# Dense weight products of a transformer block: plain fp32 in place of three fp32r products on split halves

## The chip, the cores and the metric

The kernel runs on one core of one Trainium2 chip, as one launch. The metric is the device time of that launch in microseconds, lower is better. TensorE (PE) multiplies, VectorE (DVE) and ScalarE (ACT) move and compute elementwise, GpSimd (POOL) does small work and issues the gathers, SyncE (SP) issues the weight loads.

## The reference

One transformer block, batch 1, 256 tokens, width 2048, all in fp32:

```python
xn = rms_norm(x, norm_mix_g); z = xn @ w_in            # 2048 x (5632 + 48 + 4096)
# differential attention (8 heads) and NSA attention (16 heads) on z, gated
h  = x + mix(o_da @ w_branch_da, o_nsa @ w_branch_nsa, gates) @ w_out
h += memory_cross_attention(rms_norm(h), rms_norm(mem), w_xq, w_xkv, w_xo)
q  = rms_norm(h) @ peer_wq                              # 2048 x 2048
e  = top 16 of 16384 experts for each of 256 tokens and 8 heads
out = rms_norm(h + sum_k softmax(score) * gelu(U[e_k] . xn) * V[e_k])
```

The dense products are `x @ w_xkv, w_in, w_branch_*, w_out, w_xq, w_xo, peer_wq`; the expert rows U[e] and V[e] are gathered from memory.

## The kernel before

Tokens are on partitions in two halves (C = 2 of 128). A dense product is cut into output tiles of 512 columns (NW), and a tile into eight pieces (PIECES) of 256 rows of the weight, 512 KB each; a piece holds KS = 2 blocks of 128 rows. So a tile takes 8 x 2 x 2 = 32 products of a 128x128 stationary operand (the transposed activations) with 128x512 weights. The tiles are numbered: `T_KV` (2 tiles, memory keys and values), `T_QKV` (11), `T_NG` (one narrow tile of 48 columns), `T_BG` (8, branch gates), `T_BR` (4), `T_WO` (4), `T_XQ` (1): 30 full tiles, 960 products. The tiles of `w_xo` and `peer_wq` that follow are already multiplied as plain fp32, straight from the landed pieces (`xo_pass`, L1098; `h0_piece`, `h1_piece`; `raw_tile_piece`, L1174).

For the 30 tiles SP loads each piece into `wraw`, a ring of WR = 4 slots (L416). ACT copies it to fp32r, the high half (`hi`, L1322); DVE subtracts that from the raw piece, the low half (`lo`, L1753); both go to the ring `ws`, AHEAD = 3 pieces before they are used. The activations are kept as a pair as well: after the transposes on PE, ACT writes the high and DVE the low half into `orr`, `xr` or `xr2` (L1335 and L1762, `mix_hi`/`mix_lo`, `x2_hi`/`x2_lo`). PE then makes each product from three fp32r matmuls into one bank, in `part`:

```python
nc.tensor.matmul(dst, hi, w_h, start=..., stop=False)   # L749
nc.tensor.matmul(dst, hi, w_l, start=False, stop=False) # L750
last = nc.tensor.matmul(dst, lo, w_h, ...)              # L751
```

`xq_piece` (L1029 to L1031) and the narrow tile (L818 to L820) do the same. Order is by program order of each engine and semaphores: `w_landed` (a slot has its piece), `w_hi` and `w_split` (halves made), `w_used` (PE has done with a piece, both token halves). SP's next load into a slot waits for `w_split`; ACT's `hi` waits for `w_used`.

The stages follow each other on PE: the memory tiles, the 11 projection tiles, the narrow tile and the compression (L829), attention, whose small matmuls (L851, L858, L867, L727, L932) alternate with the pieces of the eight gate tiles (`fill`), the branch tiles, `w_out` with the residual on DVE (L2032), the cross-attention query `T_XQ`, cross attention and `w_xo`, `peer_wq`, and last the expert phase: gathers of U rows (L604) for dot products on DVE (L2252) and of V rows (L613) for matmuls with a diagonal (`v_slot`, L1205).

Of the kernel before, what the change touches and what calls it, by code (L numbers as in the profile page):

```python
# [32 lines left out]
F32R = mybir.dt.float32r  # L33
# [12 lines left out]
WR = 4  # L46
AHEAD = 3
MIX_AFTER = 2
EPS = 1e-6
# [35 lines left out]
H_MEM, H_X, H_OT, H_MIX, H_X2, H_OX, H_X3 = 0, 8, 16, 24, 32, 40, 42  # L85
# [75 lines left out]
def block_program(nc, x, mem, positions, norm_mix_g, w_in, lq1, lk1, lq2, lk2, subln_g, cmp_pos, ck1, ck2,  # L161
# [3 lines left out]
    with ctx:  # L165
# [21 lines left out]
        ws = at_kb("ws", 16, [P, WR, 2, KS, NW], F32R)  # L187
        xr = at_kb("xr", 48, [P, 2, KT, S], F32R)
# [3 lines left out]
        orr = at_kb("orr", RES_KB, [P, 2, KT, S], F32R)  # L192
        xr2 = at_kb("xr2", 80 + 32, [P, 2, KT, S], F32R)
# [139 lines left out]
        w_hi, w_split, w_used = sem("w_hi"), sem("w_split"), sem("w_used")  # L333
        hi_done = sem("hi_done")
# [64 lines left out]
        def _(sp):  # L399
# [313 lines left out]
        def _(pe):  # L713
# [96 lines left out]
            for n in range(PIECES):  # L810
                pe.wait_ge(w_split, T_NG * PIECES + n + 1 + WR)
                if n == 0:
                    pe.wait_ge(acc_free[0], T_NG + 1)
                for k in range(KS):
                    kk = n * KS + k
                    w_h, w_l = (ws[:, n % WR, t, k, 0:NG_COLS] for t in range(2))
                    dst = B[0][0:NG_COLS, 0:S]
                    nc.tensor.matmul(dst, w_h, xr[:, 0, kk, :], start=(kk == 0), stop=False)  # L818
                    before = nc.tensor.matmul(dst, w_h, xr[:, 1, kk, :], start=False, stop=False)
                    last = nc.tensor.matmul(dst, w_l, xr[:, 0, kk, :], start=False, stop=(kk == KT - 1))  # L820
                if n == PIECES - 1:
                    before.then_inc(acc0_ready, 1)
# [147 lines left out]
            def branch_part(i, n, groups=None):  # L970
                if n < 4:
                    part(i + T_BR, i + T_BR, n, orr[:, :, 0:8, :], final=3, groups=groups)
                else:
                    part(i + T_BR, i, n, orr[:, :, 8:16, :], bank=4, first=4, groups=groups)
# [45 lines left out]
            def xq_piece(n, c):  # L1020

                if c == 0:
                    pe.wait_ge(w_split, T_XQ * PIECES + (n + 1 + WR))
                if n == 0:
                    pe.wait_ge(acc_free[c], T_XQ + 1)
                for k in range(KS):
                    x_h, x_l = (xr2[:, t, n * KS + k, c * P:(c + 1) * P] for t in range(2))
                    w_h, w_l = (ws[:, n % WR, t, k, :] for t in range(2))
                    nc.tensor.matmul(B[c], x_h, w_h, start=(n == 0 and k == 0), stop=False)  # L1029
                    nc.tensor.matmul(B[c], x_h, w_l, start=False, stop=False)  # L1030
                    last = nc.tensor.matmul(B[c], x_l, w_h, start=False, stop=(n == PIECES - 1 and k == KS - 1))  # L1031
# [10 lines left out]
            for n in range(WR):  # L1042
# [6 lines left out]
            for n in range(WR, PIECES):  # L1049
# [159 lines left out]
            xq_piece(WR, 1)  # L1209
            xq_piece(WR + 1, 1)  # L1210
            qx_transposes(0)
            xq_piece(WR + 2, 1)
# [5 lines left out]
            xq_piece(WR + 3, 1)  # L1218
# [78 lines left out]
        def _(act):  # L1297
# [5 lines left out]
            act.sem_inc(w_split, WR)  # L1303
# [20 lines left out]
            def next_cols(n, cols, following):  # L1324

                return cols if n + AHEAD < PIECES else following

# [4 lines left out]
            def evac_hi(n, number, dst):  # L1332

                act.wait_ge(tp_ready[n % 2], n // 2 + 1)
                A(dst, four(n), ACT.Copy).then_inc(hi_done, 1)  # L1335

# [3 lines left out]
            def quarter_hi(base, q, dst):  # L1340
                for c in range(C):
                    evac_hi(base + 2 * q + c, 0, dst[:, 0, 4 * q:4 * q + 4, c * P:(c + 1) * P])
# [19 lines left out]
            hi(-3, 0)  # L1362
            quarter_hi(G_MEM, 0, orr)
            hi(-2, 0)
            quarter_hi(G_MEM, 1, orr)
            hi(-1, 0)
            for k in range(PIECES - 1):
                hi(k, T_KV)
                if k in (1, 3):
                    quarter_hi(G_MEM, 2 + k // 2, orr)  # L1370
                if k in (4, 5):
                    squares(k - 4, ssq[:, k - 4:k - 3], mn[:, k - 4, :], square_a)
            for c in range(C):
                copy_acc(c, T_KV, T_KV, stage_a[:, c, :], 0)
            hi(PIECES - 1, T_KV)
# [3 lines left out]
            for k in range(PIECES):  # L1379
                hi(k, T_KV + 1)  # L1380
                if k == 1:
                    for c in range(C):
                        evac(G_MK + c, kxT[:, :, c * P:(c + 1) * P], four(G_MK + c))
                if 2 <= k < 6:
                    quarter_hi(G_X, k - 2, xr)
                if k in (3, 4):
                    for q in range(4):
                        act.wait_ge(x_landed[q], 16)
                    squares(2 + k - 3, ssq[:, 2 + k - 3:3 + k - 3], xn[:, k - 3, :], square_a)
# [5 lines left out]
            def qkv_tile(i):  # L1395
                for n in range(PIECES):
                    hi(n, i + T_QKV)
# [9 lines left out]
            for last in range(T_CMP + 2 - T_QKV, N_QKV):  # L1407
                for n in range(PIECES):
                    hi(n, T_QKV + last, next_cols(n, NW, NG_COLS) if last == N_QKV - 1 else NW)
# [3 lines left out]
            for n in range(PIECES):  # L1413
                hi(n, T_NG, next_cols(n, NG_COLS, NW))
            acc_wait(1, T_NG, T_NG)
            A(gnT[:, :], B[0][0:NG_COLS, 0:S], ACT.Copy).then_inc(acc_free[0], 1)
            act.sem_inc(acc_free[1], 1)
# [13 lines left out]
            A(lamb[:, 2:4], lamb[:, 0:2], ACT.Exp).then_inc(lam_exp, 1)  # L1431

# [24 lines left out]
            with act.Fori(0, N_G) as g:  # L1457
                for j in range(2):
# [12 lines left out]
                    tile = step + T_BG  # L1471
                    exps(U[0], 0, nks[0])
                    exps(U[1], 1, nks[1])
                    hi(0, tile)
                    copy_pt(U[0], 0, nt[0])
                    hi(1, tile)
# [4 lines left out]
                    hi(2, tile)  # L1481
                    exps(U[3], 3, nks[3])
                    copy_pt(U[2], 2, nt[2])
                    hi(3, tile)
# [4 lines left out]
                    hi(4, tile)  # L1489
                    exps(U[5], 5, nks[5])  # L1490
                    copy_pt(U[4], 4, nt[4])
                    hi(5, tile)
                    copy_pt(U[5], 5, nt[5])
                    hi(6, tile)
                    hi(7, tile)
# [4 lines left out]
            def mix_hi(i):  # L1500
                for c in range(C):
# [3 lines left out]
            for n in range(PIECES):  # L1505
                if n < 4:
                    quarter_hi(G_OT, n, orr)
                hi(n, T_BR)
            with act.Fori(1, N_BR) as i:
                for n in range(PIECES):  # L1510
                    if n == MIX_AFTER:
                        mix_hi(i - 1)
                    hi(n, i + T_BR)
            for n in range(PIECES):
                if n == MIX_AFTER:
                    mix_hi(N_BR - 1)
                hi(n, T_WO)
            def x2_hi(i):
                for c in range(C):
                    act.wait_ge(tp_ready[c], i + (G_X2 // 2 + 1))  # L1520
                    A(xr2[:, 0, bass.ds(i * 4, 4), c * P:(c + 1) * P], four(c), ACT.Copy).then_inc(hi_done, 1)

            with act.Fori(1, N_WO - 1) as i:
                for n in range(PIECES):
# [868 lines left out]
```

## Time and profile before

| | us |
|---|---|
| median of 3 timed runs (2191.33 to 2194.05) | 2192.86 |
| span of the profiled execution, first to last instruction | 2192.2 |
| PE busy in it | 1887.3 |
| DVE busy | 1292.6 |
| ACT busy | 583.2 |
| mean DMA rate | 320 GB/s |

The profiled execution's span is 0.66 us under the median, and the record gives no other time for it, so sums made against the span are read as sums against the median too. An interval between two instructions' starts tells how long one holds PE; a matmul's own duration is longer, since matmuls are pipelined and their ends are modelled. Busy time is a union of such durations.

### The profile page before, as it was taken

How to read it: one execution, taken by the hardware profiler on the slowest of the kernel's cores; microseconds unless marked ns; L12 is line 12 of the kernel's file. 1: busy time of each engine (PE TensorE's matmuls, PEld its weight loads, DVE VectorE, ACT ScalarE, POOL GpSimd, SP SyncE). 2: the span in 40 equal slices, each digit the busy share in tenths (PEclk: the TensorE clock that was granted, in tenths of full speed). 3: DMA queues.
4: the chain of work that ended last, by engine and by line, in shares of the span. 5: the costliest groups of instructions: out<-in, count | busy, mean ns of one | idle time of the engine just before them, and what ended most of it. 6: DMA issues, size and time to landing. Idle time of an engine off the chain costs nothing.

```text
span 2192.2 us, 22286 instructions
## 1 busy us (share of the span) xinstructions
PE 1887.3 (86%) x6607; PEld 1118.5 (51%) x6607; DVE 1292.6 (59%) x2173; ACT 583.2 (27%) x1058; POOL 716.3 (33%) x621
## 2 busy tenths in 40 slices
PE   8999999999999999999987777777777777777776
PEld 7888887777788886544433222222222222222222
DVE  6554557777766554876365566466466556556444
ACT  5544445455544442121111111111111111111101
POOL 1000101010000001445464454455455455455542
PEclk9999999999999999999999999999999999999999
DMA  8667744343456665999999999999999999999997
GB/s 295 182 177 207 229 141 116 115 115 115 124 169 211 213 226 194 391 413 412 411 412 421 421 422 422 422 422 422 422 421 422 421 422 421 423 421 422 422 421 328
DMA packets 163553, 700.86 MB, mean 320 GB/s; under 512 B 15616, under 2 KB 23840, under 8 KB 97200
## 3 DMA queue, kind: packets, MB, share of 16 engines
q0 software_dynamic: 74144, 537.32, 59.1%
q1 hardware_dynamic: 89216, 162.68, 23.7%
q8 instruction: 24, 0.39, 0.1%
q10 hardware_dynamic: 144, 0.26, 0.0%
q14 instruction: 25, 0.20, 0.0%
HBM read 698.11 MB, written 2.10 MB: 319 GB/s over the span
## 4 chain that ended last, share of the span: by engine, by line
PE 53%; DMA 37%; issue 4%; DVE 3%; POOL 1%; ACT 1%; POOLq 0%; DVEq 0%; SPq 0%; ACTq 0%
DMA v_ring<-in_peer_v_dram,idx_v 29%; PE banks L1205 11%; PE banks L749 10%; PE banks L751 9%; PE banks L750 9%; DMA big<-in_peer_u_dram,idx_u 6%; PE banks L1174 4%; DVE big L2252 2%; PE banks L867 2%; PE banks L727 1%; PE banks L851 1%; DMA wraw<-in_w_xkv_dram 1%; PE banks L858 1%; POOL v_ring L613 1%; PE banks L1117 1%
## 5 line engine op out<-in xcount | busy, mean ns | idle before, releaser
L1205 PE MATMUL banks<-v_ring,kxT 128*128 128x512 f32 x1920 | 887.2, 606 | 271.5 <-DMA v_ring<-in_peer_v_dram,idx_v 267.1
L2252 DVE SCALAR_TENSOR_TENSOR big<-big,xn 128x2048 f32<-128x2048 f32 x256 | 586.8, 2292 | 411.9 <-DMA big<-in_peer_u_dram,idx_u 403.5
L1205 PEld LDWEIGHTS banks<-v_ring,kxT 128*128 128x128 f32 x1920 | 349.5, 191 | 806.5 <-ACT kxT L1659 391.7
L604 POOL DMA_INDIRECT big<-in_peer_u_dram,idx_u x256 | 357.7, 1397 | 235.1 <-DVE big L2252 140.6
L613 POOL DMA_INDIRECT v_ring<-in_peer_v_dram,idx_v x240 | 286.3, 1193 | 388.6 <-PE banks L1205 347.0
L1753 DVE TENSOR_TENSOR ws<-wraw,ws 128x1024 fp32r<-128x1024 f32 (+1 forms) x248 | 294.8, 1195 | 189.7 <-ACT ws L1322 187.5
L1659 ACT ACTIVATE kxT<-ident,ga 128x128 f32<-128x128 f32 x240 | 95.4, 401 | 962.6 <-PE banks L1205 955.7
L1322 ACT ACTIVATE ws<-wraw 128x1024 fp32r<-128x1024 f32 (+1 forms) x248 | 254.8, 1032 | 226.1 <-PE banks L751 203.8
L749 PE MATMUL banks<-ws,xr 128*128 128x512 f32 x736 | 294.3, 400 | 0.9 <-DVE h L2032 0.9
L751 PE MATMUL banks<-ws,xr 128*128 128x512 f32 x736 | 287.3, 390 | 0.0
L750 PE MATMUL banks<-ws,xr 128*128 128x512 f32 x736 | 286.6, 389 | 0.0
L749 PEld LDWEIGHTS banks<-ws,xr 128*128 128x128 f32 x736 | 138.2, 188 | 33.2 <-issue 2.7
L751 PEld LDWEIGHTS banks<-ws,xr 128*128 128x128 f32 x736 | 138.1, 188 | 30.1
L750 PEld LDWEIGHTS banks<-ws,xr 128*128 128x128 f32 x736 | 138.4, 188 | 26.9
L559 POOL TENSOR_TENSOR rstd<-msq,nhalf 128x1 f32<-128x1 f32 x9 | 5.0, 558 | 314.2 <-DVE msq L1740 220.7
L593 POOL TENSOR_TENSOR ms<-ms,nhalf 128x2 f32<-128x2 f32 x8 | 5.5, 690 | 244.6 <-DVE ms L1939 244.6
L749 PE MATMUL banks<-ws,orr 128*128 128x512 f32 x192 | 76.5, 398 | 5.1 <-DVE orr L1762 2.4
L751 PE MATMUL banks<-ws,orr 128*128 128x512 f32 x192 | 75.0, 390 | 0.0
L750 PE MATMUL banks<-ws,orr 128*128 128x512 f32 x192 | 74.7, 389 | 0.0
L570 POOL COPY att<-big 128x256 f32<-128x256 f32 x8 | 5.8, 767 | 194.5 <-DVEq L1881 194.5
L2259 DVE TENSOR_TENSOR ga<-act_u,gw 128x16 f32<-128x16 f32 x16 | 2.8, 175 | 106.2 <-ACT act_u L1653 106.2
L1438 ACT ACTIVATE att<-att,nmx 128x128 f32<-128x128 f32 (+1 forms) x96 | 42.7, 446 | 56.3 <-DVE nmx L1906 56.3
(301 smaller groups left out, 1538.4 us busy)
## 6 DMA issues: line engine op xcount, KB each, us to landing
wraw<-in_w_in_dram SPq DMA_DIRECT2D x152, 512.0 KB, 3.7
wraw<-in_w_out_dram SPq DMA_DIRECT2D x32, 512.0 KB, 4.0
wraw<-in_w_xkv_dram SPq DMA_DIRECT2D x16, 512.0 KB, 7.0
wraw<-in_w_branch_da_dram SPq DMA_DIRECT2D x16, 512.0 KB, 3.7
wraw<-in_w_branch_nsa_dram SPq DMA_DIRECT2D x16, 512.0 KB, 4.2
wq<-in_peer_wq_dram SPq DMA_DIRECT2D x16, 512.0 KB, 21.1
wraw<-in_w_xq_dram SPq DMA_DIRECT2D x8, 512.0 KB, 3.6
wb<-in_peer_wq_dram SPq DMA_DIRECT2D x8, 512.0 KB, 8.0
```

Source lines behind the costliest of these rows:

```text
L604: nc.gpsimd.indirect_dma_start(u_ring[:, r, :], None, peer_u[0], bass.IndirectOffsetOnAxis(ap=idx_u[par][:, j:j + 1], axis=0)).then_inc(u_ ...
L613: nc.gpsimd.indirect_dma_start(v_ring[:, r, :], None, peer_v[0], bass.IndirectOffsetOnAxis(ap=idx_v[par][:, j:j + 1], axis=0)).then_inc(v_ ...
L749: nc.tensor.matmul(dst, hi, w_h, start=(n == first and k == 0), stop=False)
L750: nc.tensor.matmul(dst, hi, w_l, start=False, stop=False)
L751: last = nc.tensor.matmul(dst, lo, w_h, start=False, stop=(n == final and k == KS - 1))
L867: last = nc.tensor.matmul(dst, a, v, start=(n == 0), stop=(n == len(terms) - 1))
L1174: last = nc.tensor.matmul(B[c], xf[:, n * KS + k, c * P:(c + 1) * P], raw_pieces[raw_slot(g)][:, k, :], start=(n == 0 and k == 0), stop=(n ...
L1205: last = nc.tensor.matmul(V_BANKS[c][n], diag[:, r, :], v_ring[:, r, n * NW:(n + 1) * NW], start=(first and j == 0), stop=(final and j == ...
L1322: A(ws[:, q % WR, 0, :, 0:cols], wraw[:, q % WR, :, 0:cols], ACT.Copy).then_inc(w_hi, 1)
L1659: A(diag[:, j % RING, :], ident[:, :], ACT.Copy, scale=ga[:, par, j:j + 1]).then_inc(diag_ready, 1)
L1753: V.tensor_tensor(ws[:, q % WR, 1, :, 0:cols], wraw[:, q % WR, :, 0:cols], ws[:, q % WR, 0, :, 0:cols].bitcast(F32), ALU.subtract).then_in ...
L2252: V.scalar_tensor_tensor(out=u_ring[:, r, :], in0=u_ring[:, r, :], scalar=1.0, in1=xn3[:, par, :], op0=ALU.mult, op1=ALU.mult, accum_out=d ...
```

## The change

All halves go. `xr`, `orr` and `xr2` hold one fp32 copy; ACT evacuates the transposes of the first token half and DVE those of the second. `ws` is gone, and `wraw` takes its room as a ring of eight slots, one for each piece of a tile. PE waits for `w_landed` itself and makes each product with one plain fp32 matmul from `wraw`. SP's load into a slot waits for `w_used` of the piece eight before. The pieces of `w_xo`, which land in the same room, each wait for the `T_XQ` piece of the same number to be used for both token halves. The gate tiles' second accumulator is now handed over after `rope_done`. `XQ_BOTH = 4` keeps the order of the query tile that WR gave before.

```diff
-WR = 4
-AHEAD = 3
+WR = PIECES
+XQ_BOTH = 4
...
-        ws = at_kb("ws", 16, [P, WR, 2, KS, NW], F32R)
-        xr = at_kb("xr", 48, [P, 2, KT, S], F32R)
+        xr = at_kb("xr", 48, [P, KT, S])
...
             def load(n, tile, src, cols=NW):
-                sp.wait_ge(w_split, tile * PIECES + (n + 1))
+                sp.wait_ge(w_used, tile * PIECES + (n + 1))
                 sp.dma_start(wraw[:, n % WR, :, 0:cols], src).then_inc(w_landed[n % WR], 16)
...
-            for i in range(WR):
-                sp.wait_ge(w_split, T_XQ * PIECES + WR + i + 1 + WR)
-                xo_piece(i)
-            for i in range(WR, PIECES):
-                sp.wait_ge(w_used, T_XQ * PIECES + WR + (i - WR) // 2 + 1 + WR)
+            for i in range(PIECES):
+                sp.wait_ge(w_used, T_XQ * PIECES + WR + i + 1)
                 xo_piece(i)
...
-                pe.wait_ge(w_split, tile * PIECES + (n + 1 + WR))
+                pe.wait_ge(w_landed[n], tile * 16 + 16)
...
                     for k in range(KS):
-                        hi, lo = (lhs[:, t, (n - first) * KS + k, c * P:(c + 1) * P] for t in range(2))
-                        w_h, w_l = (ws[:, n % WR, t, k, 0:cols] for t in range(2))
-                        dst = B[bank + c][:, 0:cols]
-                        nc.tensor.matmul(dst, hi, w_h, start=(n == first and k == 0), stop=False)
-                        nc.tensor.matmul(dst, hi, w_l, start=False, stop=False)
-                        last = nc.tensor.matmul(dst, lo, w_h, start=False, stop=(n == final and k == KS - 1))
+                        last = nc.tensor.matmul(B[bank + c][:, 0:cols], lhs[:, (n - first) * KS + k, c * P:(c + 1) * P], wraw[:, n, k, 0:cols],
+                                                start=(n == first and k == 0), stop=(n == final and k == KS - 1))
...
-            def hi(n, tile, cols=NW):
-                q = n + AHEAD
-                act.wait_ge(w_landed[q % WR], tile * (16 * PIECES // WR) + 16 * (q // WR + 1))
-                act.wait_ge(w_used, tile * PIECES + (q + 1))
-                A(ws[:, q % WR, 0, :, 0:cols], wraw[:, q % WR, :, 0:cols], ACT.Copy).then_inc(w_hi, 1)
...
+            act.wait_ge(rope_done, 2)
+            act.sem_inc(acc_free[1], 1)
...
-            def mix_hi(i):
-                for c in range(C):
-                    act.wait_ge(tp_ready[c], i + (G_MIX // 2 + 1))
-                    A(xr[:, 0, bass.ds(i * 4, 4), c * P:(c + 1) * P], four(c), ACT.Copy).then_inc(hi_done, 1)
+            def mix_0(i):
+                act.wait_ge(tp_ready[0], i + (G_MIX // 2 + 1))
+                A(xr[:, bass.ds(i * 4, 4), 0:P], four(0), ACT.Copy).then_inc(tp_free[0], 1)
...
-            def lo(n, tile, cols=NW):
-                q = n + AHEAD
-                dve.wait_ge(w_hi, tile * PIECES + (q + 1))
-                V.tensor_tensor(ws[:, q % WR, 1, :, 0:cols], wraw[:, q % WR, :, 0:cols], ws[:, q % WR, 0, :, 0:cols].bitcast(F32),
-                                ALU.subtract).then_inc(w_split, 1)
...
+            def quarter_1(base, q, dst):
+                n = base + 2 * q + 1
+                dve.wait_ge(tp_ready[1], n // 2 + 1)
+                V.tensor_copy(dst[:, 4 * q:4 * q + 4, P:S], B[3].rearrange("p (t s) -> p t s", t=4)).then_inc(tp_free[1], 1)
```

Every call of `hi` and `lo` is deleted with them. Nothing from `xo_pass` on changes.

## Rows read from the trace of the kernel before

**Rows 1.** Page, part 4: shares of the chain that ended last, by line.
```profile
DMA v_ring<-in_peer_v_dram,idx_v 29%; PE banks L1205 11%; PE banks L749 10%; PE banks L751 9%; PE banks L750 9%; DMA big<-in_peer_u_dram,idx_u 6%; PE banks L1174 4%; DVE big L2252 2%; PE banks L867 2%; PE banks L727 1%; PE banks L851 1%; DMA wraw<-in_w_xkv_dram 1%; PE banks L858 1%; POOL v_ring L613 1%; PE banks L1117 1%
```

**Rows 2.** Busy time by stage; columns: stretch and length, engines, clock, DMA share, GB/s.
```profile
11.00:41.40 30.40, 25.80 (x123) 20.59 (x123) 18.88 (x24) 15.59 (x20) 1.10 (x2) 1.00 1.02 347
41.40:67.90 26.50, 26.43 (x137) 22.27 (x137) 20.80 (x29) 18.94 (x25) 0.00 (x0) 1.00 0.54 160
67.90:309.80 241.90, 241.33 (x1073) 199.80 (x1072) 123.83 (x149) 108.52 (x117) 6.85 (x10) 1.00 0.64 190
309.80:325.90 16.10, 15.08 (x135) 14.62 (x134) 8.56 (x34) 9.46 (x20) 4.65 (x6) 1.00 0.73 232
325.90:607.80 281.90, 281.55 (x1545) 221.16 (x1544) 209.62 (x557) 149.98 (x357) 23.98 (x42) 1.00 0.40 116
607.80:703.40 95.60, 95.60 (x462) 80.15 (x462) 61.70 (x73) 40.76 (x46) 0.00 (x0) 1.00 0.58 181
703.40:796.60 93.20, 91.84 (x418) 75.02 (x417) 54.26 (x58) 41.09 (x45) 0.00 (x0) 1.00 0.65 215
796.60:821.90 25.30, 25.28 (x119) 21.01 (x120) 10.99 (x17) 9.87 (x20) 1.08 (x2) 1.00 0.84 275
821.90:900.00 78.10, 71.62 (x302) 50.34 (x301) 44.83 (x104) 19.26 (x51) 15.56 (x13) 0.96 0.65 244
```

**Rows 3.** Page, part 5: the two operations that make the weights' halves.
```profile
L1753 DVE TENSOR_TENSOR ws<-wraw,ws 128x1024 fp32r<-128x1024 f32 (+1 forms) x248 | 294.8, 1195 | 189.7 <-ACT ws L1322 187.5
L1322 ACT ACTIVATE ws<-wraw 128x1024 fp32r<-128x1024 f32 (+1 forms) x248 | 254.8, 1032 | 226.1 <-PE banks L751 203.8
```

**Rows 4.** PE's instructions in order of time, steady projection tiles, first and last.
```profile
119.80 0.39 PE L750 MATMUL banks<-ws,xr 128*128 128x512 f32 x1
...
125.92 0.39 PE L750 MATMUL banks<-ws,xr 128*128 128x512 f32 x1
```

**Rows 5.** Groups by line and form on PE: records of fp32r and of plain fp32.
```profile
L749 PE MATMUL banks<-ws,xr 128*128 128x512 f32 x736 | 294.3, 400 | 0.9 <-DVE h L2032 0.9
L749 PE MATMUL banks<-ws,orr 128*128 128x512 f32 x192 | 76.5, 398 | 5.1 <-DVE orr L1762 2.4 <-ACT big L1354 1.6 <-DVE ws L1753 1.1
...
L1098 PE MATMUL banks<-wq,big 128*128 128x512 f32 x64 | 28.2, 594 | 0.0
...
L1029 PE MATMUL banks<-ws,xr 128*128 128x512 f32 x32 | 12.9, 403 | 0.4 <-DVE h L2032 0.4
```

**Rows 6.** Chain that ended last, in order of time: start, length, what.
```profile
315.64 7.10 PE banks L829 x64
...
892.85 3.45 PE banks L1145 x16
...
908.62 20.62 PE banks L1174 x48
```

**Rows 7.** PE's instructions in order of time, the edges of one attention fill.
```profile
354.62 0.39 PE L751 MATMUL banks<-ws,xr 128*128 128x512 f32 x1
354.94 0.43 PE L867 MATMUL banks<-vc,att 15*128 x2
355.30 0.66 PE L867 MATMUL banks<-big,att 128*128 x4
355.80 0.61 PE L858 MATMUL banks<-ident,att 128*128 128x128 f32 x4
356.16 0.47 PE L749 MATMUL banks<-ws,xr 128*128 128x512 f32 x1
356.48 0.39 PE L750 MATMUL banks<-ws,xr 128*128 128x512 f32 x1
```

**Rows 8.** DMA issues: kind, count, size, median us from issue to landing.
```profile
wraw<-in_w_in_dram SPq DMA_DIRECT2D x152, 512.0 KB, 3.7
...
h<-in_x_dram SPq DMA_DIRECT2D x1, 2048.0 KB, 8.9
```

More of the change, by code:

```diff
@@ L191, in block_program @@
         big = at_kb("big", 80, [P, BIG])
[L192 to L193 removed]
+        orr = at_kb("orr", RES_KB, [P, KT, S])
+        xr2 = at_kb("xr2", 80 + 32, [P, KT, S])
         mng_t = at_kb("mng", 48, [P, C, D])
@@ L815, in _ @@
                     kk = n * KS + k
[L816 to L822, printed above, removed]
+                    last = nc.tensor.matmul(B[0][0:NG_COLS, 0:S], wraw[:, n, k, 0:NG_COLS], xr[:, kk, :], start=(kk == 0), stop=(kk == KT - 1))
+                    if n == PIECES - 1 and k == 0:
+                        last.then_inc(acc0_ready, 1)
                 last.then_inc(w_used, 1)
@@ L971, in branch_part @@
                 if n < 4:
-                    part(i + T_BR, i + T_BR, n, orr[:, :, 0:8, :], final=3, groups=groups)
+                    part(i + T_BR, i + T_BR, n, orr[:, 0:8, :], final=3, groups=groups)
                 else:
-                    part(i + T_BR, i, n, orr[:, :, 8:16, :], bank=4, first=4, groups=groups)
+                    part(i + T_BR, i, n, orr[:, 8:16, :], bank=4, first=4, groups=groups)
             def x2_transposes(i):
@@ L1026, in xq_piece @@
                 for k in range(KS):
[L1027 to L1031, printed above, removed]
+                    last = nc.tensor.matmul(B[c], xr2[:, n * KS + k, c * P:(c + 1) * P], wraw[:, n, k, :],
+                                            start=(n == 0 and k == 0), stop=(n == PIECES - 1 and k == KS - 1))
                 if c == 1:
@@ L1040, in qx_transposes @@
                 transposes(G_QX + c, [(stage_b[:, c, t * P:(t + 1) * P], t * P) for t in range(X_H)])
-            for n in range(WR):
+            for n in range(XQ_BOTH):
                 if n == MIX_AFTER:
@@ L1048, in _ @@
                     xq_piece(n, c)
-            for n in range(WR, PIECES):
+            for n in range(XQ_BOTH, PIECES):
                 if n % 2 == 0:
@@ L1359, in evac @@
                 A(dst, src, ACT.Copy).then_inc(tp_free[n % 2], 1)
[L1362 to L1372, printed above, removed]
+            for q in range(4):
+                quarter_0(G_MEM, q, orr)
+            for c in range(C):
+                squares(c, ssq[:, c:c + 1], mn[:, c, :], square_a)
             for c in range(C):
                 copy_acc(c, T_KV, T_KV, stage_a[:, c, :], 0)
-            hi(PIECES - 1, T_KV)
             for c in range(C):
@@ L1378, in _ @@
                 act.sem_inc(act_steps, 1)
[L1379 to L1389, printed above, removed]
+            for c in range(C):
+                evac(G_MK + c, kxT[:, :, c * P:(c + 1) * P], four(G_MK + c))
+            for q in range(4):
+                quarter_0(G_X, q, xr)
+                act.wait_ge(x_landed[q], 16)
+            for c in range(C):
+                squares(2 + c, ssq[:, 2 + c:3 + c], xn[:, c, :], square_a)
             for c in range(C):
@@ L1509, in _ @@
-            with act.Fori(1, N_BR) as i:
[L1510 to L1521, printed above, removed]
@@ new lines, in _, with x2_0 @@
+            for q in range(4):
+                quarter_0(G_OT, q, orr)
+            with act.Fori(1, N_BR) as i:
+                mix_0(i - 1)
+            mix_0(N_BR - 1)
+            def x2_0(i):
+                act.wait_ge(tp_ready[0], i + (G_X2 // 2 + 1))
+                A(xr2[:, bass.ds(i * 4, 4), 0:P], four(0), ACT.Copy).then_inc(tp_free[0], 1)
+            with act.Fori(1, N_WO - 1) as i:
+                x2_0(i - 1)
+            x2_0(N_WO - 2)
+            act.wait_ge(h_done, 2 * N_WO - 2)
@@ L1543, in x_query @@
+            for c in range(C):
+                squares_h(2, c, False)
+            x2_0(N_WO - 1)
+            for c in range(C):
+                act.wait_ge(h_done, 2 * N_WO - 1 + c)
+                squares_h(2, c, True)
             def x_query(c):
@@ L1777, in x_gain @@
                 gain_quarter(xn, xg, gmix, q)
[L1779 to L1797 removed]
+            for q in range(4):
+                mem_gain(q)
+                quarter_1(G_MEM, q, orr)
+            for c in range(C):
+                mean_square(0, c, 1 + c)
+            x_gain(0)
             dve.wait_ge(tp_ready[0], G_POS // 2 + 1)
@@ L1802, in _ @@
             V.tensor_copy(keysT[:, :, :].rearrange("p t n -> p (t n)"), B[3][:, 0:2 * P]).then_inc(tp_free[1], 1)
-            for n in range(PIECES):
-                lo(n, T_KV + 1)
-                if n < 3:
-                    x_gain(n + 1)
-                if 2 <= n < 6:
-                    quarter_lo(G_X, H_X, xr, n - 2)
+            for q in range(4):
+                if q < 3:
+                    x_gain(q + 1)
+                quarter_1(G_X, q, xr)
             dve.wait_ge(small_landed, 16 * N_SMALL)
@@ new lines, in _ @@
+                    for t in range(2):
+                        for c in range(C):
+                            dve.wait_ge(tp_free[c], (G_CMP + 2 * t + c) // 2 + 2)
+                        for odd in range(2):
+                            rows = slice(64 * odd, 64 * odd + 64)
+                            for lh in range(2):
+                                seen = xsT[rows, t, :, 16 * lh:16 * lh + 240].rearrange("p g (n l o) -> p o l g n", o=2, l=8)[:, odd]
+                                place = posT[rows, 16 * lh:16 * lh + 16].rearrange("p (l o) -> p o l", o=2)[:, odd]
+                                last = V.tensor_tensor(blk[rows, t, 8 * lh:8 * lh + 8, :, :], seen,
+                                                       place.unsqueeze(2).unsqueeze(3).broadcast_to([64, 8, N_G, N_CMP]), ALU.add)
+                        last.then_inc(blk_ready, 1)
@@ L1881, in _ @@
                     dve.sem_inc(rope_done, 1)
-                if tiles == N_QKV:
-                    for n in range(PIECES - AHEAD, PIECES):
-                        lo(n, T_NG, NW)
             for c in range(C):
@@ L1978, in compressed_out @@
                         last.then_inc(cp_ready, 1)
-                    tile = step + T_BG
-                    SM(0), SM(1), difference(0), compressed_in(), difference(1), lo(0, tile), SM(2), lo(1, tile)
-                    EV(0), SM(3), lo(2, tile), EV(1), compressed_out(), SM(4), lo(3, tile)
-                    SM(5), EV(2), lo(4, tile), EV(3), lo(5, tile), head_norm(), EV(4), lo(6, tile), lo(7, tile), EV(5)
+                    SM(0), SM(1), difference(0), compressed_in(), difference(1), SM(2)
+                    EV(0), SM(3), EV(1), compressed_out(), SM(4)
+                    SM(5), EV(2), EV(3), head_norm(), EV(4), EV(5)
                 link.end(N_G)
             def branch_tile(i):
-                for c in range(C):
-                    for n in range(2 * c, 2 * c + 2):
-                        if isinstance(i, int):
-                            quarter_lo(G_OT, H_OT, orr, n)
-                        elif n == MIX_AFTER:
-                            mix_lo(i - 1)
-                        lo(n, i + T_BR)
+                if isinstance(i, int):
+                    for q in range(4):
+                        quarter_1(G_OT, q, orr)
+                else:
+                    mix_1(i - 1)
                 for c in range(C):
@@ L2002, in branch_tile @@
                                            op0=ALU.add, op1=ALU.mult).then_inc(acc_free[c], 1)
-                    lo(4 + c, i + T_BR)
-                for n in range(6, PIECES):
-                    lo(n, i + T_BR)
                 for c in range(C):
@@ L2046, in _ @@
                 branch_tile(i)
-            for n in range(PIECES):
-                if n == MIX_AFTER:
-                    mix_lo(N_BR - 1)
-                lo(n, T_WO)
+            mix_1(N_BR - 1)
             dve.wait_ge(h_landed, 16)
@@ L2054, in _ @@
             with dve.Fori(1, N_WO) as i:
-                for n in range(PIECES):
-                    if n == MIX_AFTER:
-                        x2_lo(i - 1)
-                    lo(n, i + T_WO)
+                x2_1(i - 1)
                 residual(i)
-            for n in range(PIECES - AHEAD):
-                if n == MIX_AFTER:
-                    x2_lo(N_WO - 1)
-                lo(n, T_XQ)
+            x2_1(N_WO - 1)
             mean_squares_h(2)
```

131 lines of the change are left out of this document (15 added, 116 removed).

## The prediction

> **What bounds the kernel now.** I read the page's chain of waits first [rows 1]. Two things fill it: the gathers of the last phase, and the three lines of the fp32r products (L749 to L751, 28% of the span together). The split lines L1753 and L1322 are not among its larger shares. So the question is what PE does before the gathers begin. The busy time by stage answers it [rows 2]: from 41.4 to 821.9 us PE's busy time falls short of the length by 3.4 us in all, and the granted clock is 1.00, which is the higher level, 2.4 GHz. Only the first stretch has idle time worth naming (4.6 us), and there the DMA runs at 347 GB/s. The DVE and ACT columns of the same rows are far from full. What they do for a piece, 1.195 us on DVE and 1.032 us on ACT [rows 3], is hidden behind the piece's twelve fp32r matmuls on PE: ACT waited 203.8 us for PE's L751 and DVE 187.5 us for ACT, so the split chain waits for PE and not the reverse. I conclude that taking the splits away frees engines that set nothing, and that the time follows what a product costs on PE.
>
> **The product, before.** In the steady stretch 27 matmuls lie between the starts 119.80 and 125.92 [rows 4]; 6.12 / 27 = 0.2267 us each, three to a product: 0.680 us. The durations of 0.39 overlap and are not the cost. A tile is 32 products, 21.76 us; eleven tiles make 239.4 us, and the projection stage lasts 241.9 with a few transposes in it [rows 2]. The price holds over the stage.
>
> **The product, after.** The kernel has the new form already, in the last dense tiles: same stationary 128x128, same 512 columns, two k blocks a piece. The trap is in the counting. `xo_pass` makes 8 x 4 = 32 products in the code, and the trace has 64 records of its line L1098 [rows 5]; L749, one fp32r matmul, has 736 records for 23 tiles x 32 products. So one plain fp32 matmul is two records. The chain shows 48 records of L1174 in 20.62 us with nothing between them [rows 6]: 0.4296 us a record, 0.859 us a product. A product thus goes from 0.680 to 0.859 us, +0.179.
>
> The Trainium skill, in "FP8 and Floating Point Precision", section "TensorE Precision Notes", says that true fp32 takes four passes through the array. At one column a cycle and 2.4 GHz that is an estimate of 4 x 512 / 2.4 = 853 ns for a product; by that rule, the trace agrees (859). A second page prices it differently and is weighed among the rivals.
>
> **The sum, stage by stage.** Full tiles hold 736 + 192 + 32 = 960 products [rows 5].
>
> - First memory tile. 32 x 0.179 = +5.7. Taken away are PE's waits ahead of L749 on `orr` (2.4), on ACT's copy of the accumulator (1.6) and on `ws` (1.1) [rows 5], 5.1 in all: the operands' evacuation is one copy on each of two engines in place of two steps in a row, the squares on ACT no longer stand behind splits, and a landed piece needs no split. The loads keep their place in SP's queue behind the same quarters of `mem`, so they land no later; at 347 GB/s they can't land much earlier either. Net +0.6. Bounds: +5.7 if another wait replaces these, 0 if all are gone and the slower PE hides a little more.
> - Second memory tile, 11 projection, 8 gate, 4 branch, 4 output tiles and the query tile: 29 x 32 = 928 products, all in stages where PE has no idle time to absorb them: 928 x 0.179 = +166.1.
> - Narrow tile. It runs from 309.8 [rows 2] to about 315.5, before L829 at 315.64 [rows 6]: 5.7 us for 16 products of 256 columns. Plain fp32 at 256 columns is 3.45 us for 16 records [rows 6], 0.216 each; 32 records make 6.9. So +1.2.
> - Edges of the 64 attention fills. The gap from the last fp32r matmul to L867 is 0.32 and not 0.227, and the first matmul after the transposes holds 0.32 too [rows 7]: 0.09 at each end, at most 64 x 0.18 = 11.5 us. Part of it is the true cost of the small instruction before, and part the change of operand rows, both of which stay. I take -3, with 0 and -11.5 as the ends. Idle time that the longer fills could still hide is 0.35 us in this stage [rows 2], nothing.
> - Between the output tiles PE waits for DVE's residual L2032, 0.9 + 0.4 us [rows 5]. PE goes on with the second token half meanwhile, which grows by the same 0.179 a product, and DVE has no split in front of the residual. The wait goes, and a little of the modelled ends with it: -2. Bounds 0 and -3.
> - Copies on ACT and DVE that remain: about as many as before and half as long in sequence, behind 3.4 us pieces. Cost nothing; were that cover gone, each group of transposes would show one, half a split's 1.195 us [rows 3] for half its columns, 0.6 us.
> - Loads. PE takes 512 KB in 4 x 0.859 = 3.44 us, 153 GB/s, less than the 190 that the projection stage draws [rows 2]. A slot is refilled when PE has used it, seven pieces or 24 us before it is needed, against 3.7 us to land and 8.9 for the 2 MB of `h` [rows 8], behind which piece 7 of the first output tile still queues. Nothing late. Likewise the pieces of `w_xo`: the last is issued when the query tile ends and is used three `xo_pass` later, after 3 x 4 x 0.859 = 10.3 us and more. The broadcast behind it in SP's queue is one 512 KB piece later, inside the same slack. Hidden; if not, 1 to 3 us once.
> - Everything after 821.9 us is unchanged work in unchanged order: it moves as a block. DVE and ACT lose 295 and 255 us of busy time [rows 3], which the chain did not hold.
>
> Sum: 0.6 + 166.1 + 1.2 - 3 - 2 = +162.9. The third decimal of the product matters: two records in 0.858 in place of 0.859 take 1 us off. I round to +161. On 2192.2 us, and on the median, that is **2353.5 us**, 7.4% slower.
>
> **Rivals.**
>
> Faster, because a plain product costs 0.430 and not 0.859. If the two records were one product's two token halves, or a second record an artefact, each product would fall from 0.680 to 0.430: 960 x -0.250 = -240, 1952 us. It decides the sign from below 0.680 us a product. For it: one record alone does take 0.430. Against it: the code's count of L1098 against its 64 records [rows 5]. Two in a hundred.
> The Trainium skill, in "Perfetto Trace Analysis", section "Engine Utilization", halves the output rate of 307.2 G elements/s for fp32 low-high; read as the rate of a whole product, an estimate of 512 x 128 / 153.6 G = 427 ns, this rival's price. The trace agrees with it for one record only.
>
> The clock drops. Plain fp32 would keep PE at work without pause for 950 us, and if it were granted less for parts of that, products would double to 1.72 us there. Against it: 20.62 us of L1174 at full rate and 1.00 in every dense stage now. For it: 0.96 in the stretch 821.9 to 900 [rows 2], though that stretch holds 6.5 us of PE idling. If the dense stages fell to 0.96 the mean cost would be 960 x 0.859 x 0.04 = 33 us more: 2387. Four in a hundred.
>
> Loads or hand-overs come late. The ring now waits for PE itself, and SP's queue is one line: a late `h` load holds the next tile's pieces. Three or four waits of 4 us: +14, 2367. Against it the slack above. Four in a hundred.
>
> The fill edges and small waits give back their whole bound, as everything on PE is then one kind: -8.5 more on the edges, -1 on the residual: 2344. One in ten, and inside my range.
>
> No change, as where plain fp32 would be made of three records or be issued as before: 2192. Against it the two records. Under one in a hundred.
>
> **How the numbers follow.** My forecast has 79 in 100, with its neighbour (2344) 89. The range takes the bounds: low is 2192.2 + 0 + 166.1 + 1.2 - 11.5 - 3 - 1 (the third decimal) = 2344, taken to 2341 for the scatter between runs; high is 5.7 + 166.1 + 1.2 with nothing given back, 173, that is 2365, and reaches to 2367 for the late loads. Outside it lie the clock, the faster rival, no change and what I don't see: about one in ten. Faster by over 0.2%: 0.03, the counting rival and a little. Within 0.2%, about what a measurement of this kernel can tell from no change: 0.01. Slower: 0.96.
>
> **What would show it.** In the profile after, the line of `part` has two records for each product, 1856 over `xr` and `orr`, with starts 0.429 us apart and no wait ahead of them; the projection stage lasts 302 to 305 us; an attention step of 35.2 us takes about 40.5; the first U gather comes about 160 us later, and from there to the end nothing moves. The expert phase keeps its DMA rate. The prediction is wrong if the spacing is not 0.429 in the long stages, if the clock there is not 1.00, or if PE shows waits for `wraw`.

## The result, and the profile after

The changed kernel takes 2354.88 us (median of 4, 2354.01 to 2356.12) against 2193.01 (4 runs, 2191.33 to 2194.05): a ratio of 1.0737, interval 1.0722 to 1.0752. That is 161.9 us more, where 161 were forecast. The profiled execution spans 2351.1 us, 158.9 more than the one before; the two figures differ by the scatter of the runs, which is 2 to 3 us for either kernel.

First the chain that ended last, shares by line, the answer to [rows 1]:

```profile
PE banks L739 34%; DMA v_ring<-in_peer_v_dram,idx_v 28%; PE banks L1187 10%; DMA big<-in_peer_u_dram,idx_u 7%; PE banks L1156 4%; PE banks L852 2%; DVE big L2115 1%; PE banks L720 1%; PE banks L1012 1%; PE banks L836 1%; POOL v_ring L606 1%; PE banks L843 1%; PE banks L1080 1%; PE banks L1099 1%; PE banks L1127 0%
```

L739 is the one matmul of `part`; it stands where L749 to L751 stood with 28%, and the gathers' share has merely shrunk with the longer span. The groups on PE by line and form, beside [rows 5]:

```profile
L739 PE MATMUL banks<-wraw,xr 128*128 128x512 f32 x1472 | 647.1, 595 | 0.0
L739 PE MATMUL banks<-wraw,orr 128*128 128x512 f32 x384 | 167.6, 592 | 0.0
...
L1012 PE MATMUL banks<-wraw,xr 128*128 128x512 f32 x64 | 28.1, 592 | 0.0
```

1472 + 384 = 1856 records for 928 products: two for each, as counted. The last number, PE's idle time ahead of the line, is 0.0 in all three: PE never waits ahead of a dense product, where it waited 5.1 + 0.9 + 0.4 us before. The chain in order of time gives the price over a long stretch, beside [rows 6]:

```profile
66.15 281.55 PE banks L739 x656
```

656 records with nothing between them, 0.4292 us each, 0.858 us a product. Busy time by stage, the same stages as [rows 2] at their new places (the branch and output tiles are left out):

```profile
11.00:41.00 30.00, 30.00 (x90) 14.47 (x89) 7.55 (x14) 6.71 (x9) 1.51 (x2) 1.00 1.05 370
41.00:72.80 31.80, 31.80 (x106) 16.31 (x105) 9.90 (x30) 8.41 (x12) 1.07 (x2) 1.00 0.49 148
72.80:377.60 304.80, 304.23 (x721) 135.24 (x719) 16.18 (x44) 18.80 (x29) 2.79 (x8) 1.00 0.51 147
377.60:395.30 17.70, 16.68 (x119) 13.05 (x119) 3.55 (x26) 5.29 (x12) 1.90 (x6) 1.00 0.69 241
395.30:720.30 325.00, 324.65 (x1288) 173.99 (x1287) 137.13 (x493) 93.66 (x292) 16.54 (x42) 1.00 0.36 102
...
952.50:982.70 30.20, 30.20 (x87) 14.78 (x86) 4.42 (x11) 4.90 (x14) 1.11 (x2) 1.00 0.62 205
982.70:1060.00 77.30, 71.49 (x305) 50.32 (x304) 44.68 (x104) 19.01 (x50) 15.39 (x13) 0.96 0.68 249
```

The DVE column, the third of the busy times, shows the splits gone: 124 us in the projection stage before, 16 now; 210 and 137 in attention. PE's column fills each dense stage, as before, and each stage is longer by its products. The clock is 1.00 throughout, 2.4 GHz, and the one stretch at 0.96 is cross attention, as before; of its two longer waits the one of 3.6 us stays and the other falls from 1.5 to 0.8 us. An attention step takes 325.0 / 8 = 40.6 us, where about 40.5 were forecast, and the gathers run at 421 to 422 GB/s in most slices of either page. The first gather of U rows leaves at 859.1 us before and at 1019.6 after: +160.5. From there to the end it is 1333.1 and 1331.5 us.

### The profile page after: what moved, and what is told of

Read it like the earlier page. It is cut to its first block, busy times and chain, and to the rows that moved or that the text cites. A ratio compares the mean times of both kernels' runs of the same rounds, so it can differ in the third digit from the quotient of the medians.

```text
span 2351.1 us, 19088 instructions
## 1 busy us (share of the span) xinstructions
PE 2051.8 (87%) x5631; PEld 939.8 (40%) x5631; DVE 995.5 (42%) x1905; ACT 333.8 (14%) x790; POOL 711.7 (30%) x621
## 4 chain that ended last, share of the span: by engine, by line
PE 57%; DMA 35%; issue 4%; DVE 2%; POOL 1%; ACT 0%; POOLq 0%; DVEq 0%; ACTq 0%
PE banks L739 34%; DMA v_ring<-in_peer_v_dram,idx_v 28%; PE banks L1187 10%; DMA big<-in_peer_u_dram,idx_u 7%; PE banks L1156 4%; PE banks L852 2%; DVE big L2115 1%; PE banks L720 1%; PE banks L1012 1%; PE banks L836 1%; POOL v_ring L606 1%; PE banks L843 1%; PE banks L1080 1%; PE banks L1099 1%; PE banks L1127 0%
## 5 line engine op out<-in xcount | busy, mean ns | idle before, releaser
L739 PE MATMUL banks<-wraw,xr 128*128 128x512 f32 x1472 | 647.1, 595 | 0.0
L597 POOL DMA_INDIRECT big<-in_peer_u_dram,idx_u x256 | 363.3, 1419 | 229.7 <-DVE big L2115 138.8
L739 PEld LDWEIGHTS banks<-wraw,xr 128*128 128x128 f32 x1472 | 274.2, 190 | 323.8 <-issue 320.3
L739 PE MATMUL banks<-wraw,orr 128*128 128x512 f32 x384 | 167.6, 592 | 0.0
L739 PEld LDWEIGHTS banks<-wraw,orr 128*128 128x128 f32 x384 | 71.6, 190 | 83.7 <-issue 83.7
L1319 ACT ACTIVATE big<-banks,rstd 128x512 f32 (+1 forms) x26 | 17.9, 688 | 303.2 <-PE banks L739 291.1
L1156 PE MATMUL banks<-wq,big 128*128 128x512 f32 x128 | 56.6, 592 | 0.0
L1783 DVE SCALAR_TENSOR_TENSOR att<-banks,causal 128x256 f32<-128x256 f32 (+1 forms) x48 | 26.7, 556 | 51.5 <-PE banks L836 50.4
L1906 DVE SCALAR_TENSOR_TENSOR h<-banks,h 128x512 f32 (+1 forms) x8 | 5.5, 692 | 76.7 <-PE banks L739 76.7
L852 PE MATMUL banks<-big,att 128*128 x240 | 36.1, 281 | 0.0
```

Of the source, the lines that this page charges most:

```text
L597: nc.gpsimd.indirect_dma_start(u_ring[:, r, :], None, peer_u[0], bass.IndirectOffsetOnAxis(ap=idx_u[par][:, j:j + 1], axis=0)).then_inc(u_ ...
L739: last = nc.tensor.matmul(B[bank + c][:, 0:cols], lhs[:, (n - first) * KS + k, c * P:(c + 1) * P], wraw[:, n, k, 0:cols], start=(n == firs ...
L852: last = nc.tensor.matmul(dst, a, v, start=(n == 0), stop=(n == len(terms) - 1))
L1156: last = nc.tensor.matmul(B[c], xf[:, n * KS + k, c * P:(c + 1) * P], raw_pieces[raw_slot(g)][:, k, :], start=(n == 0 and k == 0), stop=(n ...
L1783: V.scalar_tensor_tensor(out=sv, in0=pv, scalar=ATT_SCALE, in1=mask.unsqueeze(1).broadcast_to([P, 2, nk]), op0=ALU.mult, op1=ALU.add).then ...
```

## The experiments

Runs are beside the kernel before on the same chip, whose medians were 2193.0 to 2193.8. "First gather" is the start of the first L604 (or the same statement under its new line number), the end of all that the change touches.

**The product's form alone.** The kernel before with all its splits and waits, one plain matmul on the high halves read as fp32. The narrow tile keeps its three fp32r matmuls:

```diff
-nc.tensor.matmul(dst, hi, w_h, ...); nc.tensor.matmul(dst, hi, w_l, ...); nc.tensor.matmul(dst, lo, w_h, ...)
+last = nc.tensor.matmul(dst, hi.bitcast(F32), w_h.bitcast(F32), ...)
```

> The kernel before with its splits, its rings and all its hand-overs, but each dense product is one plain fp32 matmul on the two high halves read as fp32; the low halves are still made and not used, so the low terms are left out. My theory (the product's price on TensorE is the whole change, 0.859 against 0.680 us): as slow as the changed kernel, 2353 to 2363 us, and at most 5 us above it, because the waits in the first memory tile stay. Rival (the freed VectorE and ScalarE, the eight slots and the single copies are worth something that hid part of a still dearer product): 2370 us or more.

Measured 2352.89 us (4 runs), ratio 1.0729 (1.0711 to 1.0747). The first gather leaves at 1020.2 us, 0.6 us after the changed kernel's. The groups by line on DVE and ACT show that the work is still there:

```profile
L1749 DVE TENSOR_TENSOR ws<-wraw,ws 128x1024 fp32r<-128x1024 f32 (+1 forms) x248 | 294.9, 1194 | 289.9 <-ACT ws L1318 287.6 <-DVE big L1844 1.0
```
```profile
L1318 ACT ACTIVATE ws<-wraw 128x1024 fp32r<-128x1024 f32 (+1 forms) x248 | 253.8, 1028 | 321.1 <-PE banks L749 300.1 <-DMA wraw<-in_w_xkv_dram 8.7 <-PE banks L1027 6.0
```

So 549 us of work on two engines, four raw slots and every hand-over of the pairs came back, and the time did not change by what can be measured. In the first gather this run is 0.6 us later although its narrow tile is 1.4 us shorter, so splits, pairs and ring together are worth about 2 us. Of some 160 us the form of the product is all the rest; its rival, over 2370 us, is out.

**Four fp32r products.** A fourth matmul, low times low:

```diff
+nc.tensor.matmul(dst, lo, w_h, start=False, stop=False)
+last = nc.tensor.matmul(dst, lo, w_l, start=False, stop=...)
-last = nc.tensor.matmul(dst, lo, w_h, start=False, stop=...)
```

> The kernel before with a fourth fp32r matmul, low half times low half, for each of the 960 full products. If a stage lasts as long as its matmuls: +960 x 0.2267 = +218 us, 2411 us, so four fp32r matmuls (0.907 us) come out 46 us above one plain fp32 product (0.859 us). Rival, that the split chain or the loads set the time in part: less than 200 us more.

Measured 2404.96 us (2 runs), ratio 1.0965 (1.0943 to 1.0987): +211, 7 short of the sum, and first gather +210.4. Longer pieces hide most of the waits on splits and residuals, as the plain product does: of the 6.4 us that PE idled ahead of the dense products before, 1.0 are left, on `orr`. Four fp32r matmuls cost 52 us more than one plain product in the same kernel (e1: 2352.89), by the spacings 960 x (0.907 - 0.858) = 47. Plain fp32 is about what four fp32r passes are, a little cheaper, and three of them are cheaper still.

**Two fp32r products, splits kept.** Without the low activations:

```diff
 nc.tensor.matmul(dst, hi, w_h, ...)
-nc.tensor.matmul(dst, hi, w_l, start=False, stop=False)
-last = nc.tensor.matmul(dst, lo, w_h, start=False, stop=...)
+last = nc.tensor.matmul(dst, hi, w_l, start=False, stop=...)
```

> The kernel before without the product of the low activations (two fp32r matmuls a product; that term is left out). A piece then takes 1.81 us on TensorE against 1.195 us on VectorE. My theory: the split chain is still hidden, -218 us, 1975 to 1985 us. Rival: the splits or the slot's cycle of load, high half and low half (about 3.7 + 1.0 + 1.2 us for four slots, 1.5 us a piece) set the time already: over 2000 us.

Measured 2035.11 us (2 runs), ratio 0.9279 (0.9260 to 0.9297). My expectation failed: 159 us less and not 218, and the rival's range was the right one. The groups on PE until 700 us show waits that were not there before, 27 us of them ahead of L749:

```profile
L749 PE MATMUL banks<-ws,xr 128*128 128x512 f32 x736 | 299.9, 407 | 17.6 <-DVE ws L1751 7.5 <-ACT big L1352 6.2 <-DVE h L2030 3.4
...
L749 PE MATMUL banks<-ws,orr 128*128 128x512 f32 x192 | 78.0, 407 | 9.4 <-ACT big L1352 4.0 <-DVE orr L1760 3.4 <-DVE ws L1751 2.1
```

DVE takes 1.2 us for a piece of 1.81, so its mean was no obstacle; its queue was. A chain of rotations holds it at 129 to 134 us, the split stands behind them, and PE stands behind the split. The chain in order of time has it:

```profile
133.19 0.35 DVE big L1846
133.75 1.24 DVE ws L1751
135.03 0.50 PE banks L749
```

That is one place. ScalarE's late accumulator copies (`big`) cost PE as much as the splits do (10.2 and 9.6 us). Up to the end of the query tile PE is busy for 606.9 of 654.6 us:

```profile
11.00:665.60 654.60, 606.87 (x3041) 480.18 (x3042) 502.54 (x937) 393.29 (x644) 36.73 (x62) 0.98 0.68 214
```

That is 47.7 us idle, against 8.0 in the same stages of the kernel before (802.6 of 810.6). The clock also has a part: its mean there is 0.98 and not 1.00.

**One fp32r product, splits kept.** Only `hi` times `w_h`.

> The kernel before with one fp32r matmul a product, high times high; both low terms are left out, all splits are still made. TensorE alone would save 960 x 0.453 = 435 us: 1758 us. My theory: here the split chain and the slot's cycle (load, high, low: about 1.5 us a piece) bind outside attention, and VectorE's own 210 us bind inside it: about 290 us saved, 1880 to 1930 us. Rival, that splits are always hidden: under 1800 us.

Measured 2030.93 us (2 runs, 2022.92 to 2038.93), ratio 0.9258 (0.9222 to 0.9295). With half of the matmuls of the run before it, it gains next to nothing: first gather at 705.1 us against 703.0. Far over my range. The same stages, up to the end of the query tile:

```profile
11.00:667.70 656.70, 491.34 (x2080) 355.70 (x2081) 502.64 (x937) 389.15 (x644) 36.64 (x62) 0.81 0.67 212
```

960 x 0.2267 = 218 us of matmuls were taken out against the run with two. PE's busy time fell by 115.5 us only, and its idle time rose by 117.7: ahead of L749 PE alone waits 39.4 us for DVE's splits and 39.4 for ScalarE's accumulator copies. The other 102 us came back inside PE's busy time. Some of them are modelled ends ahead of the new waits; most go with the granted clock, 0.81 on average where the run with two has 0.98. Dense matmuls start 0.427 us apart in the stretches at the lower level and 0.227 in those at the higher. An estimate from these rows: 0.38 of 656.7 us at the lower level, with PE busy for three quarters of them, cost half of 187 us, 93 us, and 12 us in the run with two. The expectation had no term for the clock. How much of it lies on the path that sets the time was not tested.

**Half the columns, no splits.** The changed kernel with 256 columns in 824 of its 960 products; half of their columns are left out:

```diff
+ends = (n == first and k == 0) or (n == final and k == KS - 1)
+half = slice(0, cols) if ends else slice(k * cols // 2, (k + 1) * cols // 2)
-last = nc.tensor.matmul(B[bank + c][:, 0:cols], lhs[...], wraw[:, n, k, 0:cols], ...)
+last = nc.tensor.matmul(B[bank + c][:, half], lhs[...], wraw[:, n, k, half], ...)
```

> The changed kernel with 256 columns in place of 512 in 824 of the 960 plain products (the first and last of each accumulation stay whole), so half of those products' columns are left out. If each of the two records goes with its columns: 824 x 0.428 = 353 us less, 2002 us, at 1.72 us a piece without any split. Rival, that the loads (512 KB in 1.72 us, 305 GB/s) set the time: over 2020 us.

Measured 2016.41 us (2 runs), ratio 0.9192 (0.9175 to 0.9209), 14 above the sum. First gather 681.7, 337.9 before the changed kernel's where 353 were worked out. PE's waits are short and scattered (4.9 us in attention, 1.1 on the loads of `w_xkv`); they don't add up to the 15, and I leave the rest open. Still, at a piece of 1.72 us the kernel without splits gives up 15 of 353 us, and the kernel with splits at 1.81 us 59 of 218.

**Weights rounded only.** The same two products' worth on PE as in the run with two, but without DVE's subtraction for the weights; their low halves are left out:

```diff
 def lo(n, tile, cols=NW):
-    V.tensor_tensor(ws[:, q % WR, 1, :, 0:cols], wraw[...], ws[...].bitcast(F32), ALU.subtract).then_inc(w_split, 1)
+    pass
...
-A(ws[:, q % WR, 0, :, 0:cols], wraw[:, q % WR, :, 0:cols], ACT.Copy).then_inc(w_hi, 1)
+A(ws[:, q % WR, 0, :, 0:cols], wraw[:, q % WR, :, 0:cols], ACT.Copy).then_inc(w_split, 1)
...
-nc.tensor.matmul(dst, hi, w_l, start=False, stop=False)
```

> The kernel before, with the weights only rounded to fp32r by ScalarE and VectorE's subtraction for them taken out; a product is two fp32r matmuls, high and low half of the activation with the rounded weight, so the weights' low halves are left out. TensorE's work is that of the run with two products, which saved 159 us where its matmuls alone were worth 218. My theory (that run lost its 59 us to VectorE's subtraction standing in line with rotations, residuals and softmax ahead of TensorE): at least 45 of them come back, 1980 to 1992 us. Rival (the slot's cycle of load and rounding, or late copies on ScalarE): 2010 us or more.

Measured 1996.64 us (4 runs), ratio 0.9096 (0.9081 to 0.9111). 38 us of the 59 came back, under my 45 and some 5 us above my range, and some 2 of them belong to the narrow tile, which lost its third product too: the first gather leaves at 661.1, 42 us before that of the run with two. The run doesn't separate DVE's queue from the cycle of a slot: without the subtraction a raw slot is also free earlier, and ScalarE's waits for landings of `w_in` fell from 38.1 to 13.7 us. What is left ahead of L749 is ScalarE's:

```profile
L749 PE MATMUL banks<-ws,xr 128*128 128x512 f32 x736 | 296.1, 402 | 3.8 <-ACT ws L1319 2.4 <-ACT vmem L1351 1.1 <-ACT big L1351 0.2
...
L749 PE MATMUL banks<-ws,orr 128*128 128x512 f32 x192 | 78.3, 408 | 4.9 <-ACT ws L1319 2.6 <-ACT big L1351 1.9 <-issue 0.4
```

**Weights rounded, one product.** All low terms left out.

> As the run before it, with one fp32r matmul a product, the high half of the activation with the rounded weight; all low terms are left out. TensorE alone: 1758 us. My theory: outside attention the loads set the time, 512 KB at 350 to 390 GB/s being 1.35 to 1.5 us a piece against 0.91 on TensorE, and in attention the softmax chain: 1840 to 1890 us. Rival (VectorE's subtraction was not what held the run with one product): 2000 us or more.

Measured 1931.10 us (4 runs), ratio 0.8805 (0.8790 to 0.8820): 100 us below the run with one product and its splits, so the subtraction did hold that one, and 41 above my range. Part of the 100 us came by way of the clock: its mean up to the end of the query tile is 0.92 here and 0.81 there. I had the next bound wrong. It was to be the loads; PE's own waits name ScalarE:

```profile
PE banks L749 <- ACT big L1349: 41.1, 10, 5.5
PE banks L749 <- ACT ws L1317: 34.8, 32, 7.6
```

These are the copies of the accumulators (`big`) and the rounding (`ws`), one engine's queue. Behind it ScalarE itself waits for landings of `w_in` for 35.4 us and of `w_out` for 20.6, so the loads have a part in it. Which of the two would give more was not tried.

**A shorter lead of the ring.** The changed kernel, loads held until four more pieces are used:

```diff
-sp.wait_ge(w_used, tile * PIECES + (n + 1))
+sp.wait_ge(w_used, tile * PIECES + (n + 1 + 4))
```

> The changed kernel with each load of the ring held until four more pieces are used, so that pieces land at most three ahead and only four slots are in use. My theory (24 us of lead were far more than the 3.6 us to land, 3 x 3.44 = 10.3 us still are): the same within 0.2%, 2351 to 2359 us. Rival, that the lead of eight slots kept the price of late loads down: 2365 us or more, with waits for the weight ring on TensorE.

Measured 2353.77 us (4 runs), ratio 1.0733 (1.0715 to 1.0750), the changed kernel's within the scatter. No wait for `wraw` appears on PE. Eight slots bring nothing here that four don't.

**Fewer waits with fp32r.** The kernel before, in another order:

```diff
-                if k in (4, 5):
-                    squares(k - 4, ...)
+                if k in (3, 4):
+                    squares(k - 3, ...)
...
 def residual(i):
     for c in range(C):
+        if c == 1:
+            lo(PIECES - 1, i + T_WO)      # was ahead of residual(i)
```

> The kernel before, with fp32r as it was, but two waits of TensorE taken out by order alone: ScalarE squares the memory rows one piece earlier (wait of 1.6 us at the second memory tile), and VectorE does the residual of the first token half before the last split of an output tile (four waits of about 0.5 us). My theory: 3 to 4 us less, 2189 us, at the edge of what can be measured; the trace shows the waits gone. Rival: the waits are taken over by another engine, same time.

Measured 2190.95 us (11 runs) against 2193.20 (15 runs), ratio 0.9994 (0.9985 to 1.0003): not told from no change. The first gather leaves at 856.7 us, 2.4 earlier. The residual's part of the theory holds, its wait of 0.9 us ahead of L749 [rows 5] is gone:

```profile
L749 PE MATMUL banks<-ws,xr 128*128 128x512 f32 x736 | 294.3, 400 | 0.0
```

The other part does not: PE still waits 1.75 us for ScalarE at the second memory tile.

```profile
40.78 0.47 PE L749 MATMUL banks<-ws,orr 128*128 128x512 f32 x1 [1.75 <-ACT big L1354]
```

## Why the prediction was right

The step that carries it is the price of a product. The stages bear out its terms one by one, each start read from PE's instructions in order of time:

| stage | forecast | measured |
|---|---|---|
| first memory tile, up to the second's start (41.47 to 41.01) | +0.6 | -0.5 |
| second memory tile, projections (to 309.85; to 377.65) | +68.7 | +68.3 |
| narrow tile (to 315.48; to 384.69) | +1.2 | +1.4 |
| compression, up to attention (10.4; 10.6) | 0 | +0.2 |
| attention with 256 fill products (281.9; 325.0) | +45.8 - 3 | +43.1 |
| branch and output tiles (188.8; 231.6) | +45.8 - 2 | +42.8 |
| query tile (25.0; 30.5) | +5.7 | +5.5 |
| after it (1370.6; 1368.6) | 0 | -2.0 |

The stages up to the end of the query tile add up to +160.9, the forecast's terms to +162.8, taken to 161 for the third decimal. That the medians differ by 161.9 is partly luck: the profiled executions differ by 158.9, and the first tile, the output tiles and the end each came out about 1 to 2 us under their terms.

**Product.** 0.858 in place of 0.859 us; the form run shows by itself that this is the change.

**First memory tile.** The waits are gone, and with them a little more than their modelled length: -0.5 lies just outside the bounds of 0 and +5.7. In the form run, where the operands' pairs stay, the wait for `orr` is 1.05 us again and the tile starts at 11.70 against 10.37:

```profile
11.70 3.67 PE L749 MATMUL banks<-ws,orr 128*128 128x512 f32 x8 [1.05 <-DVE orr L1758]
```
```profile
10.37 3.60 PE L739 MATMUL banks<-wraw,orr 128*128 128x512 f32 x8
```

The first line is the form run's, the second the changed kernel's, both from PE's instructions in order of time. The 1.3 us are what the single copies bring there. The reasons given for the rest were not needed. The form run keeps the pairs, the splits and the squares behind them, and yet the second wait for `orr` (1.35 us before), the one for `ws` (1.1) and the one for ACT's accumulator copy (1.6) are gone from it too: a longer product hides them. Nor was 347 GB/s the limit of the loads; the changed kernel draws 370 in this stretch. The form run is no slower at the end than the changed kernel, within scatter.

**Fill edges.** I took 3 of at most 11.5 us. Measured are 2.6: 256 products at the measured 0.178 us are 45.7, and the stage grew by 43.1. The number was right, and where it came from was not. The gap ahead of the attention matmuls [rows 7] stays with plain fp32 on both sides, here as 3.53 us between a fill's start and L852, where its eight records take 3.43:

```profile
425.43 3.60 PE L739 MATMUL banks<-wraw,xr 128*128 128x512 f32 x8
428.96 0.43 PE L852 MATMUL banks<-vc,att 15*128 x2
```

The words on the change of rows hold. A plain record ahead of work on 15 or 64 rows (L852 on `vc`, L836) holds PE 0.52 us and one ahead of work on all 128 rows its steady 0.43; fp32r held 0.32 and 0.23 in the same places, so 0.09 stays in either form. The other edge was in part no cost. Behind transposes the first fp32r matmul held 0.314 us, but the last transpose ahead of it held 0.028 and now holds 0.109: the time has only moved to another instruction. So the edges gave back less than 0.5 us of the 3. The other 2.1 were inside the fills: the 640 fp32r matmuls there started 0.230 us apart on average and not the 0.2267 that the forecast carried over from the projection stage, while plain records keep 0.4292. Why fp32r is slower there was not tested.

**Residual.** The wait went, as forecast, and the stage gave back 2.9 us against 45.7, within the bounds of 0 and -3. In the form run, where DVE still has a split in front of the residual, it is gone too, so the longer second token half is enough.

**Cover.** That the splits lay behind PE was right at 2.72 us a piece, but for the one wait of 1.1 us in the first tile, and the form run shows it at 3.43. But the words "frees engines that set nothing" rested partly on mean times, and that reasoning doesn't carry far: at 1.81 us a piece, with the same 1.2 us a piece on DVE, 59 of the 218 us did not come, and without the subtraction 38 of them did.

**Loads and the rest.** Nothing late, with either lead. The clock rival did not come: 1.00 in every dense stage under 960 x 0.858 = 824 us of plain fp32 products. The faster rival needed one record a product; there are two.

No version here beats both kernels at the same arithmetic. The two runs with rounded weights are faster by 9.0% and 12.0%, and they buy it with terms of the product.

## What to carry to other kernels

Count a line's records against the code's instructions before you price a matmul: a plain fp32 product is two records, 0.858 us at 512 columns, and three fp32r matmuls at 0.680 beat it as long as making the halves stays hidden. Work that is hidden now is worth nothing when it is taken away, and a mean below the bound does not tell how long it stays hidden: an engine that runs its queue in order makes it late in bursts, behind whatever stands ahead. When TensorE's work shrinks, look for the next wait in the in-order queues of the helpers as well as in the bandwidth, and look at the granted clock: of the 218 us taken out of the run with one product some 80, by the estimate above, came back as slower matmuls.

## What the runs showed of the hardware

Four fp32r matmuls in a row (4 x 0.2267 = 0.907 us) take longer than one plain fp32 product (2 x 0.4292 = 0.858 us). The Trainium skill, in "FP8 and Floating Point Precision", section "TensorE Precision Notes", counts four passes for true fp32; by that count an estimate for a pass in the plain form is 0.2146 us, 5% less than an fp32r matmul of its own. No run here shows the passes themselves, only two records a product. Taking the second fp32r matmul away while the splits stay moved the first gather by +2 us and not down, with a mean granted clock of 0.81 up to the end of the query tile; PE idled there for 165.4 of 656.7 us. Between small matmuls of attention, fp32r matmuls start 0.230 us apart and not 0.2267; plain fp32 records keep 0.4292 in both places.
